# Expert sums left in four PSUM banks of a fused transformer kernel, and a rearranged head and end of its expert stage

## The reference, cut to what matters

```python
logits = ht @ w_router + b_router
top_val, top_idx = lax.top_k(logits, 4)
gates = jax.nn.softmax(top_val, axis=-1)
# blocks of 128 (token, expert) pairs, one expert e per block:
hg = xblk @ w_gu[e] + b_gu[e]
x_glu = jnp.minimum(hg[:, :1024], 7.0)
x_lin = jnp.clip(hg[:, 1024:], -7.0, 7.0)
act = x_glu * jax.nn.sigmoid(1.702 * x_glu) * (x_lin + 1.0)
yb = act @ w_down[e] + b_down[e]
y = sum over the four experts of a token: gate * yb
out = x + gate_f * rms_norm(y, g_post_ffn)
```

## Time and profile before

| | us |
|---|---|
| median of 3 runs (lowest, highest) | 2367.19 (2366.9, 2371.65) |
| the profiled execution's own time | 2368.39 |
| its span, first to last instruction | 2366.6 |
| TensorE busy in the span | 2272.3 (96%) |
| VectorE busy | 673.7 (28%) |
| ScalarE busy | 381.2 (16%) |
| mean DMA rate over the span | 254 GB/s |

### The profile page before, as it was taken

How to read it: one execution, slowest core, us unless ns; L and a number is a source line. 1 busy time by engine, 2 the same in 40 slices (tenths; PEclk the granted TensorE clock), 3 DMA queues, 4 the chain that set the end, 5 groups by cost and what they waited for, 6 DMA issues and landing times.

```text
span 2366.6 us, 25898 instructions
## 1 busy us (share of the span) xinstructions
PE 2272.3 (96%) x10937; PEld 1477.7 (62%) x10937; DVE 673.7 (28%) x1325; ACT 381.2 (16%) x686; POOL 135.3 (6%) x191
## 2 busy tenths in 40 slices
PE   8999999999999999999999999999999999999995
PEld 6887788888878888888777733333334433333332
DVE  3344422334264132335244411111111111111112
ACT  3321122100024121000232400000000000000001
POOL 0013300000000000000000000000000000000000
PEclk9999999999999999999999999999999999999998
DMA  6220062333542335347533189999999899999994
GB/s 240 106 73 36 2 232 107 143 133 142 227 178 107 142 142 214 134 159 288 201 119 113 68 370 428 426 428 428 425 428 418 366 379 427 427 427 427 427 427 178
DMA packets 43323, 600.08 MB, mean 254 GB/s; under 512 B 5232, under 2 KB 5504, under 8 KB 6688
## 3 DMA queue, kind: packets, MB, share of 16 engines
q1 hardware_dynamic: 43200, 598.36, 62.0%
HBM read 597.29 MB, written 1.05 MB: 253 GB/s over the span
## 4 chain that ended last, share of the span: by engine, by line
PE 84%; DMA 11%; DVE 2%; ACT 1%; issue 0%; SPq 0%; PEldq 0%; DVEq 0%; ACTq 0%
PE pb L402 83%; DMA ring<-in_gu 6%; DMA arena<-in_dne 5%; PE pb L412 2%; DMA arena<-in_dn 1%; DVE arena L319 0%; DVE arena L304 0%; ACT arena L363 0%; ACT xs L363 0%; ACT xt L363 0%; DVE ring L319 0%; DMA col<-in_cols 0%; SPq L540 0%; PEldq L3032 0%; DVE xt L304 0%
## 5 line engine op out<-in xcount | busy, mean ns | idle before, releaser
L402 PE MATMUL pb<-arena 128*64 128x512 f32 (+8 forms) x2316 | 681.9, 451 | 11.7 <-DMA ring<-in_gu 8.8
L402 PE MATMUL pb<-ring,arena 128*64 128x512 f32 x1648 | 480.9, 595 | 1.7 <-DMA ring<-in_dne 1.6
L402 PE MATMUL pb<-xt,ring 128*128 128x256 f32 (+3 forms) x1808 | 402.5, 383 | 3.8 <-DVE xt L319 3.6
L402 PEld LDWEIGHTS pb<-arena 128*64 128x64 f32 (+4 forms) x2316 | 274.4, 157 | 186.2 <-issue 168.3
L402 PEld LDWEIGHTS pb<-xt,ring 128*128 128x128 f32 (+3 forms) x1808 | 339.2, 189 | 62.4 <-issue 7.6
L402 PE MATMUL pb<-kv,arena 128*64 128x512 f32 (+2 forms) x592 | 265.2, 604 | 35.1 <-DMA arena<-in_dne 34.4
L402 PEld LDWEIGHTS pb<-ring,arena 128*64 128x64 f32 x1648 | 153.0, 137 | 202.5 <-issue 202.5
L402 PEld LDWEIGHTS pb<-kv,arena 128*64 128x64 f32 (+1 forms) x592 | 88.3, 154 | 196.8 <-issue 194.3
L369 ACT ACTIVATE arena<-pb 128x512 f32<-128x512 f32 (+2 forms) x131 | 74.4, 568 | 614.6 <-PE pb L412 415.3
L304 DVE TENSOR_TENSOR mix<-pb,mix 128x512 f32<-128x512 f32 x68 | 47.1, 692 | 429.9 <-PE pb L402 429.6
L363 ACT ACTIVATE arena<-arena 128x512 f32<-128x512 f32 (+4 forms) x151 | 86.5, 573 | 296.8 <-DVE arena L319 269.1
(11 more groups left out here) (180 smaller groups left out, 1954.2 us busy)
## 6 DMA issues: line engine op xcount, KB each, us to landing
ring<-in_gu SPq DMA_DIRECT2D x67, 2048.0 KB, 18.9
arena<-in_gu SPq DMA_DIRECT2D x48, 2048.0 KB, 16.6
ring<-in_dne SPq DMA_DIRECT2D x32, 2048.0 KB, 13.8
arena<-in_dne SPq DMA_DIRECT2D x18, 2048.0 KB, 17.5
kv<-in_gu SPq DMA_DIRECT2D x17, 2048.0 KB, 15.5
kv<-in_dne SPq DMA_DIRECT2D x16, 2048.0 KB, 13.0
ring<-in_up SPq DMA_DIRECT2D x13, 2048.0 KB, 7.9
ring<-in_ada SPq DMA_DIRECT2D x9, 2048.0 KB, 8.2
```

The source lines that it names most:

```text
L402: r = self.e.matmul(out, lhsT, rhs, start=start, stop=stop, skip_group_check=True)
```

## The change

- **Sums in PSUM.** The output tiles of the jobs go round banks 0 to 3. Banks 4 to 7 hold the four quarters of the sum: `biases_p` opens them (start, no stop) and every `scatter_p` adds to them (`start=False`). `scatter_v` and the copies into `Y` are gone. `ats`, `ys` and the sigmoid's buffer `sg` become single.
- **Moved.** `biases_p` goes into job e0 (behind the turn of its first half), `back_p` and `back_s` into job e2 (`REST_AT`). The count is loaded in job e6 (`COUNT_AT`), by TensorE, ScalarE and VectorE.
- **Barrier.** `joined` stands inside the condition of round 1. GpSimd takes no part; TensorE alone increments `s_join` behind its branch.
- **End.** ScalarE loads the table of Ln and Exp ahead of the last job's turn. ScalarE and VectorE read the four banks in opposite order (`end_s`, `end_v`), VectorE multiplying by the gain at once; the final multiply-add is one instruction for each half of the tokens, and each half is stored by its own DMA.

```diff
         def biases_p(P):
+
             P.wait_ge("load b_down16")
             for i, half in TURNS:
-                b = P.tile(f"mo.y{i}{half}")
+                b = P.occupy(f"mo.y{i}{half}", Y_BANK + 2 * i + half)
                 P.wait_ge("free mo.gtt")
-                P.mm(b, GTT[0:32, i * 128:(i + 1) * 128], BDOWN[:, half * 512:half * 512 + 512], True, True,
+                P.mm(b, GTT[0:32, i * 128:(i + 1) * 128], BDOWN[:, half * 512:half * 512 + 512], True, False,
                      sig=f"mo.y{i}{half}")
...
         def scatter_p(P, n, q):
+            P.wait_ge(f"free {n}.d1")
             for i, half in TURNS:
-                b = P.tile(f"{n}.z{i}{half}")
-                P.wait_ge(f"free {n}.d1")
-                P.mm(b, SCT[q][:, i * 128:(i + 1) * 128], ys[q][:, half * 512:half * 512 + 512], True, True,
-                     sig=f"{n}.z{i}{half}")
-
-        def scatter_v(V, n):
-            for i, half in TURNS:
-                b = V.tile(f"{n}.z{i}{half}")
-                o = Y[:, i, half * 512:half * 512 + 512]
-                V.tt(o, b, o, ADD)
-                V.free(f"{n}.z{i}{half}")
+                P.mm(P.banks[Y_BANK + 2 * i + half], SCT[q][:, i * 128:(i + 1) * 128],
+                     ys[:, half * 512:half * 512 + 512], False, True, sig=f"{n}.z" if i + half == 2 else None)
...
             route_p(P, 0, JOBS[0])
-            biases_p(P)
-            back_p(P, HT, "mo.r")
+            P.main, P.i = list(range(Y_BANK)), 0
...
                 def second():
                     turn_act_p(P, n, 0)
+                    if at == 0:
+                        biases_p(P)
+                    if at == REST_AT:
+                        back_p(P, HT, "mo.r")
                     if late is not None:
                         scatter_p(P, late, 1 - q)
                     if at + 1 < len(JOBS):
                         route_p(P, 1 - q, JOBS[at + 1])
                     if at == PICK_AT:
                         pick_p(P, 0)
+                    if at == COUNT_AT:
+                        count_of(P)
...
-            last, q = JOBS[-1], (len(JOBS) - 1) % 2
-            turn_act_s(S, last, q, 1)
-            contract_s(S, last, q)
+                up_s(S, n, 1, f"{n}.a0")
+            S.table(LNEXP)
+            turn_act_s(S, JOBS[-1], 1)
+            contract_s(S, JOBS[-1])
...
         def rounds(lane, body):
-            lane.joined("moe.end", LANES)
             lane.begin("round")
-            count = None
-            if lane.e is not None:
-                lane.wait_ge("mo.ni")
-                count = lane.e.value_load(NI[0:1, 15:16], min_val=0, max_val=15)
+            before = dict(lane.seen)
             with ExitStack() as asked:
                 for r in range(1, ROUNDS):
                     if lane.e is not None:
-                        asked.enter_context(lane.e.If(count > r))
+                        asked.enter_context(lane.e.If(counts[lane.kind] > r))
+                    if r == 1:
+                        lane.joined("moe.end", LANES)
                     body(r)
                     lane.ge(lane.last)
...
+        def summed(lane):
+            lane.wait_ge(f"{JOBS[-1]}.z")
+            if lane.e is not None:
+                lane.e.wait_ge(sems("s_join"), 1)
+
+        def end_s(S):
+            summed(S)
+            for n, (i, half) in enumerate(TURNS):
+                if i:
+                    S.wait_ge(f"end.y{i}{half}")
+                S.act(XS[:, i, half * 512:half * 512 + 512], S.banks[Y_BANK + n], ACT.Square,
+                      accum=SQS[:, 2 * half + i:2 * half + i + 1])
+                S.mark(f"end.q{i}{half}")
+            S.wait_ge("end.s")
+            S.act(STMP, SS, ACT.Ln, scale=1.0 / D, bias=EPSC)
+            S.act(RS, STMP, ACT.Exp, scale=-0.5)
+            S.mark("end.e")
+
+        def end_v(V):
+            summed(V)
+            for i, half in ((1, 0), (1, 1), (0, 0), (0, 1)):
+                o = slice(half * 512, half * 512 + 512)
+                if i == 0:
+                    V.wait_ge(f"end.q{i}{half}")
+                V.tt(YP[:, i, o], V.banks[Y_BANK + 2 * i + half], PG[:, o], MUL)
+                V.mark(f"end.y{i}{half}")
+            V.wait_ge("end.q11")
+            V.tt(SS, SQS[:, 0:2], SQS[:, 2:4], ADD)
+            V.mark("end.s")
+            V.ts(STQ, SS, 1.0 / D, EPS, MUL, ADD)
+            V.wait_ge("end.e")
...
+            for i in range(2):
+                V.stt(HTOK[:, i, :], YP[:, i, :], RS[:, i:i + 1], HTOK[:, i, :], MUL, ADD)
+                V.mark(f"post.h{i}")
```

More of the change, by code:

```diff
@@ L2637, in build @@
         xgs = [AR.get(8, 128) for _ in range(2)]
-        ats = [AR.get(8, 128) for _ in range(2)]
+        ats = AR.get(8, 128)
         SELP = [AR.get(128) for _ in range(2)]
@@ L2642, in build @@
         SCT = [AR.get(256) for _ in range(2)]
-        tmp = [[AR.get(512) for _ in range(3)] for _ in range(2)]
-        ys = [MT_[:, 0:1024], MT_[:, 1024:2048]]
+        tmp = [[AR.get(512) for _ in range(2)] for _ in range(2)]
+        sg = AR.get(512)
+        ys = MT_[:, 0:1024]
         cnt, cum, st = NOV[:, 0, :], NOV[:, 1, :], NOV[:, 2, :]
@@ L2649, in build @@
         ROUNDS = 15
+        counts = {}
         PAIRS = NEXP // 2
@@ L2796, in moe_head_v @@
             V.memset(SLR, 0.0)
-            for i, half in TURNS:
-                b = V.tile(f"mo.y{i}{half}")
-                V.copy(Y[:, i, half * 512:half * 512 + 512], b)
-                V.free(f"mo.y{i}{half}")
         def slots_of(n):
@@ L2878, in up_v, with up_s @@
             V.mark(f"{n}.a{k}")
-        def up_s(S, n, k):
-            t1, t2, sg = tmp[k]
+        def up_s(S, n, k, before):
+            if before is not None:
+                S.wait_ge(before)
             S.wait_ge(f"free {n}.h{k}0")
-            S.act(sg, t1, ACT.Sigmoid, scale=1.702)
+            S.act(sg, tmp[k][0], ACT.Sigmoid, scale=1.702)
             S.mark(f"{n}.sg{k}")
@@ L2891, in turn_act_p, with turn_act_s, contract_p @@
                 P.tr(b[:, c * 128:(c + 1) * 128], a[:, c * 128:(c + 1) * 128], ident, sig=f"{n}.t{k}" if c == 3 else None)
-        def turn_act_s(S, n, q, k):
+        def turn_act_s(S, n, k):
             b = S.tile(f"{n}.t{k}")
-            S.copy(ats[q][:, k * 4:k * 4 + 4, :], b.rearrange("p (c t) -> p c t", c=4))
+            S.copy(ats[:, k * 4:k * 4 + 4, :], b.rearrange("p (c t) -> p c t", c=4))
             S.free(f"{n}.t{k}")
-        def contract_p(P, n, q, count):
+        def contract_p(P, n, count):
             P.wait_ge(f"free {n}.t0", f"free {n}.t1")
@@ L2901, in contract_p, with contract_s @@
                 b = P.tile(f"{n}.d{k}")
[L2902 to L2904 removed]
+                expand_p(P, b, ats, units_of(n, f"dn{k}", count), True, f"{n}.d{k}")
+        def contract_s(S, n):
             for k in range(2):
                 b = S.tile(f"{n}.d{k}")
[L2907 removed]
+                S.copy(ys[:, k * 512:(k + 1) * 512], b)
                 S.free(f"{n}.d{k}")
         def scatter_p(P, n, q):
+            P.wait_ge(f"free {n}.d1")
             for i, half in TURNS:
[L2912 to L2922 removed]
+                P.mm(P.banks[Y_BANK + 2 * i + half], SCT[q][:, i * 128:(i + 1) * 128],
+                     ys[:, half * 512:half * 512 + 512], False, True, sig=f"{n}.z" if i + half == 2 else None)
         JOBS = [f"e{p}" for p in range(PAIRS // 2)] + ["r0"] + [f"e{p}" for p in range(PAIRS // 2, PAIRS)]
[L2925 removed]
+        REST_AT, PICK_AT, COUNT_AT = 2, 3, 6
         def experts_of(n):
@@ L2959, in moe_p @@
                 if late is not None:
-                    contract_p(P, late, 1 - q, width_of(late))
+                    contract_p(P, late, width_of(late))
                 up_p(P, n, q, 1, width_of(n), sel, second)
@@ L2963, in moe_p @@
             turn_act_p(P, last, 1)
-            contract_p(P, last, q, width_of(last))
+            contract_p(P, last, width_of(last))
             scatter_p(P, last, q)
@@ L2972, in moe_s @@
                 if late is not None:
-                    turn_act_s(S, late, 1 - q, 1)
-                up_s(S, n, 0)
+                    turn_act_s(S, late, 1)
+                up_s(S, n, 0, late and f"{late}.a1")
                 if late is not None:
-                    contract_s(S, late, 1 - q)
-                turn_act_s(S, n, q, 0)
+                    contract_s(S, late)
+                turn_act_s(S, n, 0)
+                if at == REST_AT:
+                    back_s(S, HTOK, "mo.r")
                 if at + 1 < len(JOBS):
                     route_s(S, 1 - q, JOBS[at + 1])
-                up_s(S, n, 1)
-            last, q = JOBS[-1], (len(JOBS) - 1) % 2
-            turn_act_s(S, last, q, 1)
-            contract_s(S, last, q)
+                if at == COUNT_AT:
+                    count_of(S)
+                up_s(S, n, 1, f"{n}.a0")
+            S.table(LNEXP)
+            turn_act_s(S, JOBS[-1], 1)
+            contract_s(S, JOBS[-1])
         def moe_v(V):
@@ L2990, in moe_v @@
```

(49 more changed lines are left out.)

11 lines of the change are left out of this document (7 added, 4 removed).

## The result

Five runs of the changed kernel have a median of 2355.94 us (2353.52 to 2358.36), five of the kernel before 2369.3 (2366.9 to 2375.06): a ratio of 0.994, 95% interval 0.9923 to 0.9957, 13.4 us. A second set on another occasion gave 2355.86 against 2369.97, 0.9939 (0.9925 to 0.9953). Forecast: 13.9 us. The profiled execution of the changed kernel has a span of 2351.7 us (2353.52 with what lies around it), 14.9 less than before.

A forecast was written before the change was run, and what follows sets the result against it. Arriving weights were taken to set the expert stage's pace, with one round job TensorE bound. Terms -5.5 + 2.4 + 0.2 - 5.5 - 1.5 - 2.5 - 1.5 = -13.9 gave 2354.5, as median 2353.3 us; range 2349.3 to 2360.5.

The forecast's parts named there:

- e0: First job of the expert stage: the biases moved into it were to take 3.44 us and cost +2.4 us.
- The head: Ahead of job e0: without biases and turns there, its first tile starts earlier, -5.5 us, between -6.35 and -4.7.
- The loads run dry: In job e0: the moved biases let the DMA engines run dry, +2.4 us, ends 0 and +3.4.
- Rival (1): In job e0: the loads don't run dry behind the biases, -16.3 us in all, 2350.9; chance 0.14.
- The turns in e2 and the count in e6: In two later jobs: the residual's turns cost +0.2 us, ends 0 and +1; the count's load costs 0.
- Four banks: In the jobs: output tiles going round four banks make TensorE wait for no reader, 0 us.
- Rival (3): In the jobs: the four banks bind and TensorE waits for readers, 21 us slower, 2374; chance 0.04.
- The barrier: Behind the last product: TensorE's branch runs beside the last scatter, first square earlier, -5.5 us, ends -5.6 and -1.7.
- Rival (2): Behind the last product: TensorE's branch stays on the path, -10.1 us in all, 2357.1; chance 0.20.
- `scatter_v`'s going: In the jobs: removing VectorE's 47.6 us of adds gains 0, as that engine isn't waited for.
- Rival (4): At the end: the tables are loaded again behind the condition, +2.6 us, 2355.9; chance 0.08.
- The store's term: At the very end: storing in two halves leaves only the second half's 0.5 MB, -1.5 us, ends -0.8 and -1.9.

The follow-up runs named there:

- the second profile: The unmodified changed kernel profiled again: 1037.0 us from SyncE's stand to span's end, against 1034.0 in its first profile.
- the head back: Changed kernel with biases and residual turns ahead of the first job again: 1039.7 us from SyncE's stand to span's end, against 1034.0.
- the late branch: Changed kernel with TensorE waiting for its own last product before it branches: 17.66 us from last scatter to span's end, against 14.14.
- the experiment: Changed kernel with sums in SBUF, eight banks and VectorE's adds again: 16.96 us from last scatter to span's end, against 14.14.
- the halves in e4 and e5: Changed kernel with two of the four bias products in the fifth job, two in the sixth: median 2356.75 us, against the changed kernel's 2355.86.
- the biases twice: Changed kernel with the four bias products run twice in job e0: 1040.4 us from SyncE's stand to span's end, against 1034.0.
- in e1: Changed kernel with the biases in the second job instead of e0: 1035.6 us from SyncE's stand to span's end, against 1034.0.

## Why the prediction was right, point by point

- **The head.** Foretold 5.5 between 4.7 and 6.35, measured 5.8. The place is right: h00 begins 34.56 us behind SyncE's arrival instead of 39.89, 5.3 earlier, and from h00 to the restart it is 8.16 us instead of 8.63. But the half-clock stretch stayed away from h00, and for that case the working gives 6.35, 0.5 too much: h00 came 0.4 less early than the 5.75 reckoned with, and the clock in h00 gave back 0.5, not 0.6. That the middle between the two cases came closer is luck. The clock did cost 1.7 us in two of the twelve profiles with the early head (stand 45.1 to 45.2 instead of 43.5), a gain of 4.2, below the end of 4.7; there the half-clock stretch ahead of e0's route was twice as long, and the forecast had not looked at it.
- **The loads run dry.** Right in place and size (+2.4, and 2.7 us of DMA time lost in e0), and shown: the loss goes with the biases' place and grows with their number. Rival (1) is out. What the step left out is the clock behind the biases; in the second profile it makes the loss 4.4.
- **The turns in e2 and the count in e6**: no DMA time is lost in either place, where 0.2 us and nothing were foretold.
- **Four banks.** No cost; even three cost only 3.8 us of DMA time. Rival (3) is out. The rule of the Trainium skill, "PSUM — Partial Sum Buffer", Summary: rules for kernel authors, to evacuate promptly does not decide here: with four banks held through all jobs, no DMA time was lost with the head back (17.9 us, before 18.0).
- **The barrier.** The sequencer goes ahead of its engine: the branch began at 2337.6, with d1's copy, as the forecast had it. Rival (2) is out; the late branch gives its price, 3.5 us (3.8 foretold). One sentence was thin: VectorE's branch is early only because VectorE has no z to add any more. The forecast took this for granted and gave `scatter_v`'s going 0; by the experiment 2.8 of the 5.4 us need it. And the barrier put back shows that TensorE's branch is not the only one that counts: the branches of VectorE and ScalarE behind TensorE's last product cost 4.4 us.
- **The table.** Rival (4) is out: nothing is loaded behind the branch. Without the load ahead it is 3.7 us more, where the forecast put 2.6 on two loads.
- **The end's other terms** are within 0.1 us of the measured ones. The terms given for the squares to the correction add up to 4.68 us, not 4.55, so that working gives -1.4; measured were 4.47 us. The store's term rests on 400 GB/s, which no row shows; what a single store costs more was measured as 1.2 us.
- **The total.** 13.4 us by the medians against 13.9. From SyncE's stand on it is 14.1 us in the first profile and 11.1 in the second, the difference being the clock ahead of the route and in e0; both are set against one profile of the kernel before. The forecast of 2353.3 lies 2.6 below the measured 2355.94, since it started from a median of 2367.19, which is 2369.3 with two more runs.

## What to carry to other kernels

Where loads set the pace, look for the longest stretch between two issues and compare it with the bytes in flight: here, what was moved into it was free up to that cover (the turns in e2, the halves in e4 and e5) and cost in full beyond it (the biases twice: 6.4 of 6.7 us), and the cover was smallest at the start of the stream. Reckon what you move at the half clock too, if the profile shows such stretches nearby. The branch over unused code cost about 3 to 4 us here on each engine that took it; what counts is the last thing that engine waits for in front of it. Read an engine that "isn't waited for" once more at the end of the program.

## What the runs showed of the hardware

- The branch over the unused rounds took TensorE 3.49 to 3.94 us in the 14 profiles. VectorE took about 2.9 (its branch at 2346.3, its semaphore at 2349.2 in the kernel before), 3.0 with the sums in SBUF and about 3.5 with the barrier back.
- The biases' products have 32 rows of contraction. In five of the twelve profiles in which all four stand together, the granted clock was at its half level (1.2 GHz) for 3.4 to 6.8 us during them or right behind them, with TensorE at work before: in the kernel before, with the head back, in e1, twice in e0, and in the second profile of the changed kernel. In the other seven, the first of the changed kernel among them, it was not. Stretches of the same kind stand in other places too, behind a wait of TensorE: in the changed kernel it is idle from 1473 to 1475, and the granted clock is 0.50 from 1475 to 1477. So these products are not shown to be the cause. What decides was not tried.
- When the stream of loads restarted from an empty queue, the DMA engines lost 1.5 to 1.8 us of their full rate in the first 4 us, in every profile.
- ScalarE, without the table loaded ahead, made three loads of 1.28 us behind its branch, one of them ahead of the first square; with it, none.
